# A two-layer decoder trunk on one core: two plain tile pairs per feed-forward instead of three, the rest as seven-product pairs

## The chip, the cores and the metric

One core of a Trainium2 chip runs the whole program. The metric is the device time of one execution in microseconds (us), the median of three runs. TensorE (PE) does the matmuls; VectorE (DVE) and ScalarE (ACT) make its operands and take its results; GpSimd (POOL) issues the transfers that add weights onto an SBUF tile; SyncE (SP) issues the plain loads.

## What is computed

528 tokens (16 learned ones ahead of 512) of 1024 channels go through two layers. In float32, per layer:

```python
for l in range(2):
    h = LN(a*h + 0.5*(silu(h @ wg1) * (h @ wu1)) @ wd1)
    z = h @ w_in
    y = concat(pool_mixer(z), gated_linear_attention(z)) @ w_out
    h = LN(a*h + y)
    h = LN(a*h + 0.5*(silu(h @ wg2) * (h @ wu2)) @ wd2)
```

Each feed-forward has 2816 hidden channels. The change touches the four feed-forwards alone.

## The kernel before

Everything is held transposed: channels on the 128 partitions, tokens along the free axis. x is 8 tiles of 128 channels (`KC`), the hidden side 22 tiles (`MT`). Tokens are worked on in two halves of 264 (`HALF`), in the last feed-forward 2 x 256, since there only the 512 real tokens count.

**Precision.** Each float32 operand is split in a high part, rounded to the matmul's type by a ScalarE copy, and a low part, the difference, taken by VectorE. A product is three matmuls: high x high, high x low, low x high.

**Weights** come as a stream of pieces of 128 x 1024, one for the gate and one for the up projection of a hidden tile, through raw buffers into four slots (`w_hi`, `w_lo`, `n % SLOTS`). SyncE loads a piece as soon as its buffer is free; ScalarE writes the high part (L1208) and, for the part whose low is made by a transfer, the negated high part (L1202), onto which GpSimd's transfer (L536) adds the raw weights. For the rest VectorE subtracts (L1695).

**Two ways to do a pair of a gate tile and an up tile.** Plain: 8 input tiles x 2 token halves x 3 matmuls x 2 = 96 matmuls of 264 columns; tiles 0 to 2 (`CLASSIC`) are made so. Seven-product: the gate and up weights and the two halves of channels and tokens make a 2 x 2 block matrix product, done by Winograd's form of Strassen's scheme with 7 block products in place of 8 (`fast_pair`): 7 x 4 tiles x 3 = 84 matmuls. They run in the order P1 (plain), P5, P6 (sums of weights times sums of x), P2 (plain), P7, P3, P4. Each needs additions besides. VectorE makes four sums of raw weights per pair (`w_sums`, `s_sum`), ScalarE and VectorE split them (`sum_high`, `sum_low`), and four sums of x per feed-forward (`v_sums`, `v_sum`; split by `v_high`, `v_low`). Of the running sums in PSUM, ScalarE copies P1 from one bank to the other (L1263, `p1_copied`); P6 may add onto its bank only after that. It also copies P5 (L1277) and the sum after P6 (L1282) to SBUF, and VectorE adds them back (L1753 after P7, L1766 after P3); P4 waits for the first of these adds. The down projection of the first 18 hidden tiles runs as twelve seven-product pairs (63 matmuls each), between the up pairs; for it VectorE makes four sums of each two hidden tiles (`t_sums`).

**Order.** Nothing is scheduled by a tool: each engine's program is written out, engines run in order, and semaphores hold them back. At the start of a feed-forward TensorE does tiles 0, 1 together (L619, L620, L645 as x arrives, then L655 to L657), then plain tile 2 (L609 to L611), then the pairs in `FAST_ORDER`. Meanwhile the layer norm before ends: VectorE's last step is the low part of x tile 7 (L1933), ScalarE's the full x (L1404), and x sums need all of it. `s_hi`, `s_lo` share memory with `v_sum`, so weight sums are split after the x sums.

## Time and profile before

| | |
|---|---|
| median of 3 runs | 1784.02 us (1783.56 to 1785.22) |
| span of the profiled execution | 1782.4 us |
| TensorE busy | 1770.1 us, 99% |
| VectorE busy | 1434.4 us, 80% |
| ScalarE busy | 1168.0 us, 66% |
| GpSimd busy | 340.0 us, 19% |
| DMA | 148 GB/s mean |

A timeline row gives start, duration, engine, line, operation, tiles written and read, shape, and how many instructions it merges; in brackets the idle time ahead of it and what ended that. Matmul ends are modelled, so their spacing, not their duration, tells the rate. L numbers are lines of the kernel before.

### The profile page before, as it was taken

The page shows a single profiled execution, that of the slowest core. Times are in us where ns is not written, and L with a number is a line of the kernel's source. Part 1 is how long each engine was busy: PE and PEld are TensorE (multiplying, and loading weights), DVE is VectorE, ACT ScalarE, POOL GpSimd, SP SyncE. Part 2 cuts the span into 40 slices and gives each one's busy share as a digit, 9 for nine tenths or more (in the row PEclk, how much of TensorE's full clock was granted, in tenths as well). Part 3 has the DMA queues.
Part 4 walks back from the last instruction along what each step waited for, and adds up shares of the span by engine and source line. Part 5 has one row for each costly group of instructions (what it writes and reads, how often), then busy time and mean ns, then how long its engine had stood idle before and what let it go on. Part 6 is the DMA issues. An engine that isn't in the chain of part 4 may idle for free.

```text
span 1782.4 us, 37725 instructions
## 1 busy us (share of the span) xinstructions
PE 1770.1 (99%) x14462; PEld 1733.0 (97%) x14462; DVE 1434.4 (80%) x2577; ACT 1168.0 (66%) x2047; POOL 340.0 (19%) x376
## 2 busy tenths in 40 slices
PE   9999999999999999999999999999999999999997
PEld 9999999999999999999999999999998889999996
DVE  7988888668568988888689888886785689888886
ACT  6767666574357667676576767665743577777764
POOL 2111212311011121111311111113110111111113
PEclk9999999999999999999999999999999999999999
DMA  7675766556565766766556757565665656767662
GB/s 217 141 183 129 177 141 144 150 137 141 115 138 110 170 167 148 169 138 159 145 138 145 176 129 180 134 155 139 141 142 117 147 126 149 185 133 185 133 166 72
DMA packets 112561, 263.54 MB, mean 148 GB/s; under 512 B 10752, under 2 KB 35328, under 8 KB 112384
## 3 DMA queue, kind: packets, MB, share of 16 engines
q1 hardware_dynamic: 66592, 167.86, 32.0%
q0 software_dynamic: 45504, 92.29, 30.8%
q8 instruction: 116, 1.90, 0.4%
q10 hardware_dynamic: 288, 0.98, 0.2%
q14 instruction: 61, 0.50, 0.1%
HBM read 259.00 MB, written 2.10 MB: 146 GB/s over the span
## 4 chain that ended last, share of the span: by engine, by line
PE 99%; DVE 0%; DMA 0%; ACT 0%; issue 0%; ACTq 0%; DVEq 0%
PE PS L680 21%; PE PS L682 21%; PE PS L681 21%; PE PS L655 5%; PE PS L656 4%; PE PS L657 4%; PE PS L609 3%; PE PS L611 3%; PE PS L610 3%; PE PS L619 2%; PE PS L645 2%; PE PS L620 2%; PE PS L987 2%; PE PS L808 1%; PE PS L875 0%; PE PS L902 0%
## 5 line engine op out<-in xcount | busy, mean ns | idle before, releaser
L536 POOL DMA_DIRECT2D w_lo<-in_stream x316 | 269.4, 853 | 1336.8 <-ACT w_lo L1202 1301.9
L1198 ACT ACTIVATE s_hi<-s_sum 128x512 fp32r<-128x512 f32 (+1 forms) x496 | 291.1, 588 | 154.2 <-PE PS L682 145.4
L1701 DVE TENSOR_TENSOR s_lo<-s_sum,s_hi 128x512 fp32r<-128x512 f32 (+1 forms) x496 | 294.4, 633 | 2.9 <-ACT s_hi L1198 2.6
L680 PE MATMUL PS<-v_hi,s_hi 128*128 128x264 f32 (+1 forms) x912 | 258.8, 284 | 0.0
L682 PE MATMUL PS<-v_hi,s_lo 128*128 128x264 f32 (+1 forms) x912 | 258.1, 283 | 0.0
L681 PE MATMUL PS<-v_lo,s_hi 128*128 128x264 f32 (+1 forms) x912 | 258.0, 283 | 0.0
L682 PE MATMUL PS<-x_hi,w_lo 128*128 128x264 f32 (+1 forms) x656 | 185.8, 283 | 0.0
L680 PE MATMUL PS<-x_hi,w_hi 128*128 128x264 f32 (+1 forms) x656 | 185.7, 283 | 0.0
L681 PE MATMUL PS<-x_lo,w_hi 128*128 128x264 f32 (+1 forms) x656 | 185.6, 283 | 0.0
L681 PEld LDWEIGHTS PS<-v_lo,s_hi 128*128 128x128 f32 x912 | 172.2, 189 | 0.0
L680 PEld LDWEIGHTS PS<-v_hi,s_hi 128*128 128x128 f32 x912 | 171.8, 188 | 0.0
L682 PEld LDWEIGHTS PS<-v_hi,s_lo 128*128 128x128 f32 x912 | 171.4, 188 | 0.0
L1208 ACT ACTIVATE w_hi<-raw 128x1024 fp32r<-128x1024 f32 (+2 forms) x152 | 147.1, 968 | 8.0 <-DMA raw<-in_stream 8.0
L1202 ACT ACTIVATE w_lo<-raw 128x512 fp32r<-128x512 f32 (+2 forms) x196 | 143.1, 730 | 0.0
L655 PE MATMUL PS<-x_hi,w_hi 128*128 128x264 f32 (+1 forms) x472 | 140.9, 299 | 0.1
L656 PE MATMUL PS<-x_lo,w_hi 128*128 128x264 f32 (+1 forms) x472 | 139.0, 295 | 0.0
L657 PE MATMUL PS<-x_hi,w_lo 128*128 128x264 f32 (+1 forms) x472 | 138.8, 294 | 0.0
L1263 ACT ACTIVATE PS<-PS 128x264 f32<-128x264 f32 (+1 forms) x124 | 46.3, 373 | 136.4 <-PE PS L682 136.4
L682 PE MATMUL PS<-x_hi,s_lo 128*128 128x264 f32 (+1 forms) x448 | 127.9, 286 | 0.0
L681 PE MATMUL PS<-x_lo,s_hi 128*128 128x264 f32 (+1 forms) x448 | 127.2, 284 | 0.0
L680 PE MATMUL PS<-x_hi,s_hi 128*128 128x264 f32 (+1 forms) x448 | 127.1, 284 | 0.0
L680 PEld LDWEIGHTS PS<-x_hi,w_hi 128*128 128x128 f32 x656 | 123.5, 188 | 0.0
(295 smaller groups left out, 5719.8 us busy)
## 6 DMA issues: line engine op xcount, KB each, us to landing
raw<-in_stream SPq DMA_DIRECT2D x164, 512.0 KB, 4.4
w_lo<-in_stream POOLq DMA_DIRECT2D x160, 256.0 KB, 4.6
spare<-in_stream SPq DMA_DIRECT2D x72, 512.0 KB, 6.8
w_lo<-in_stream POOLq DMA_DIRECT2D x60, 512.0 KB, 7.7
raw<-in_stream SPq DMA_DIRECT2D x48, 384.0 KB, 4.2
spare<-in_stream SPq DMA_DIRECT2D x48, 384.0 KB, 5.3
w_lo<-in_stream POOLq DMA_DIRECT2D x96, 192.0 KB, 4.8
X<-in_x_t SPq DMA_DIRECT2D x8, 264.0 KB, 5.8
```

The costliest lines, as they stand in the source:

```text
L536: pool.dma_start(w_lo[:, slot, to], stream[n // RAWS, n % RAWS, :, part], accum_op=ALU.add).then_inc(lo_added[slot], 16)
L609: nc.tensor.matmul(o, hi, rhs_hi[:, k, tok], start=first, stop=False)
L655: yield nc.tensor.matmul(o, hi, rhs_hi[:, k, tok], start=k == 0, stop=False)
L656: yield nc.tensor.matmul(o, hi, rhs_lo[:, k, tok], start=False, stop=False)
L657: yield nc.tensor.matmul(o, lo, rhs_hi[:, k, tok], start=False, stop=k == n - 1)
L680: nc.tensor.matmul(o, hi[:, w], r_hi, start=start and k == 0, stop=False, skip_group_check=True)
L681: nc.tensor.matmul(o, hi[:, w], r_lo, start=False, stop=False, skip_group_check=True)
L682: m = nc.tensor.matmul(o, lo[:, w], r_hi, start=False, stop=stop and k == last, skip_group_check=True)
L1198: nc.scalar.activation(s_hi[:, j - 1, w], s_sum[:, j - 1, w], ACT.Copy).then_inc(S["s_hi_done"], 1)
L1202: nc.scalar.activation(w_lo[:, n % SLOTS, to], of, ACT.Copy, scale=-1.0).then_inc(S["raw_neg"], 1)
L1208: nc.scalar.activation(w_hi[:, n % SLOTS, to], of, ACT.Copy).then_inc(S["raw_hi"], 1)
L1701: V.tensor_tensor(s_lo[:, j - 1, w], s_sum[:, j - 1, w], s_hi[:, j - 1, w].bitcast(F32), ALU.subtract).then_inc(S["s_lo_done"], 1)
```

## The change

`CLASSIC` goes from 3 to 2: tile 2 becomes the first up pair of the seven-product kind, and with it the slots, buffers and waits of all pieces shift by one pair. The x sums move to memory that later holds the hidden tiles (`v_sum_a`, `v_sum_b`), so that `s_hi` and `s_lo` no longer share with them. Sum 2 of x is taken with the other sign by a plain addition, and ScalarE's `scale=-1.0` and one VectorE instruction with two operations give its high and low parts the sign back. The order of both engines at the start of a feed-forward, up to the second pair, is written anew; the adds in PSUM of the first pair become `add_p5(0)` and `add_u2(0)` within it. The low parts of hidden tile 1 and its sums go to the second and third pair. Some `then_inc` that nobody waits for are dropped.

```diff
-BEHIND = 2
+BEHIND = 3
-CLASSIC = 3
+CLASSIC = 2
...
         with ExitStack() as s4:
-            v_sum = sb("v_sum", [P, 4, BAND, HALF], F32, s4)
+            s_hi = sb("s_hi", [P, 4, BLOCK], F32R, s4)
+            s_lo = sb("s_lo", [P, 4, BLOCK], F32R, s4)
...
+                v_sum_a = sb("v_sum_a", [P, 2, BAND, HALF], F32, s11)
...
+                v_sum_b = sb("v_sum_b", [P, 2, BAND, HALF], F32, s12)
...
# TensorE, ffn
                 product(3, 3, x_hi, x_lo, KC, span=span).then_inc(S["piece_done"], 1)
-                m = CLASSIC - 1
-                for j in range(2):
...
-                        for o, tok in matmul_parts(2 * (m % 2) + j, span):
-                            x = tile_products(o, tok, n % SLOTS, k, k, x_hi, x_lo, k == 0, k == KC - 1)
-                    x.then_inc(S["piece_done"], 1)
                 for i in range(FAST):
...
# ScalarE
-            def v_high(l, f, j, n):
+            def v_high(l, f, j, span):
 
                 act.wait_ge(S["v_sum_done"], 4 * (2 * l + f) + V_ORDER.index(j) + 1)
-                nc.scalar.activation(v_hi[:, j - 1, :, 0:n], v_sum[:, j - 1, :, 0:n], ACT.Copy).then_inc(S["v_hi_done"], 1)
+                nc.scalar.activation(v_hi[:, j - 1, :, 0:halved(span)[1]], v_sum(j, span), ACT.Copy,
+                                     scale=-1.0 if j == 2 else 1.0).then_inc(S["v_hi_done"], 1)
...
# ScalarE, ffn
+                v_high(l, f, 3, span)
+                v_high(l, f, 1, span)
                 act.wait_ge(S["piece_done"], FP + 1)
                 silu_of(0, span)
-                gate_high(FP + 4)
-                gate_negative(FP + 4)
-                v_high(l, f, V_ORDER[0], halved_n)
-                v_high(l, f, V_ORDER[1], halved_n)
+                gate_high(first)
+                gate_negative(first)
+                sum_high(l, f, 0, 1)
+                v_high(l, f, 2, span)
+                up_high(first + 1)
+                sum_high(l, f, 0, 2)
                 h_high(l, f, 0, span)
-                gate_high(FP + 5)
-                gate_negative(FP + 5)
+                v_high(l, f, 4, span)
+                sum_high(l, f, 0, 3)
                 act.wait_ge(S["piece_done"], FP + 3)
                 silu_of(2, span)
-                v_high(l, f, V_ORDER[2], halved_n)
-                v_high(l, f, V_ORDER[3], halved_n)
-                gate_high(first)
-                gate_negative(first)
-                h_high(l, f, 1, span)
-                up_high(first + 1)
-                sum_high(l, f, 0, 1)
-                sum_high(l, f, 0, 2)
-                act.wait_ge(S["piece_done"], FP + 5)
-                silu_of(0, span)
-                t_high(l, f, 1, span)
-                sum_high(l, f, 0, 3)
                 sum_high(l, f, 0, 4)
-                h_high(l, f, 2, span)
                 for i, (kind, a, b) in enumerate(FAST_ORDER):
...
+                    if i == 1:
+                        hidden_high(l, f, CLASSIC - 1, span)
...
# VectorE
                     elif j == 2:
                         dve.wait_ge(S["v_sum_done"], at + 1)
-                        x = V.scalar_tensor_tensor(out=v[1], in0=v[2], scalar=-1.0, in1=b11, op0=ALU.mult, op1=ALU.subtract)
+                        x = V.tensor_tensor(v_sum(2, span), v_sum(3, span), b11, ALU.add)
...
# VectorE, ffn
-                v_sums(l, f, span, (3, 1))
+                v_sums(l, f, span, (3, 1, 2))
+                w_sums(l, f, 0, (1, 3, 2))
                 classic_product(0)
-                gate_low(FP + 4)
+                v_low(l, f, span, 1)
+                sum_low(l, f, 0, 1)
+                gate_low(first)
+                w_sums(l, f, 0, (4,))
+                v_low(l, f, span, 2)
+                sum_low(l, f, 0, 2)
+                v_sums(l, f, span, (4,))
+                v_low(l, f, span, 3)
+                sum_low(l, f, 0, 3)
+                v_low(l, f, span, 4)
+                sum_low(l, f, 0, 4)
+                classic_product(1)
+
+                w_sums(l, f, 1, (1,))
+                gate_low(fast_piece(l, f, 1))
+                add_p5(0)
+                w_sums(l, f, 1, (3, 2))
+                sum_low(l, f, 1, 1)
+                add_u2(0)
+                sum_low(l, f, 1, 2)
+                w_sums(l, f, 1, (4,))
+                sum_low(l, f, 1, 3)
+                sum_low(l, f, 1, 4)
                 h_low(l, f, 0, span)
-                v_sums(l, f, span, (2, 4))
-                gate_low(FP + 5)
-                v_low(l, f, span, 1)
-                v_low(l, f, span, 2)
-                classic_product(1)
-                w_sums(l, f, 0)
-                gate_low(first)
-                v_low(l, f, span, 3)
...
+                t_sums(l, f, CLASSIC - 1, span)
                 for i, (kind, a, b) in enumerate(FAST_ORDER):
+                    if i == 0:
+                        continue
...
+                    if i == 1:
+                        h_low(l, f, CLASSIC - 1, span)
...
+                    if i == 2:
+                        t_low(l, f, CLASSIC - 1, span)
```

## Rows read from the trace of the kernel before

**Rows 1.** The page: span, busy time by engine, and the chain that ended last.
```profile
span 1782.4 us, 37725 instructions
PE 1770.1 (99%) x14462; PEld 1733.0 (97%) x14462; DVE 1434.4 (80%) x2577; ACT 1168.0 (66%) x2047; POOL 340.0 (19%) x376
...
PE 99%; DVE 0%; DMA 0%; ACT 0%; issue 0%; ACTq 0%; DVEq 0%
```

**Rows 2.** Windows: stretch, its length, busy time (count) by engine, granted clock, DMA share, GB/s.
```profile
40.56:326.17 285.61, 285.61 (x2355) 285.37 (x2354) 240.56 (x440) 195.87 (x382) 55.90 (x62) 1.00 0.67 155
28.96:40.56 11.60, 11.60 (x99) 11.60 (x97) 11.38 (x17) 9.22 (x14) 2.56 (x3) 1.00 0.75 161
1455.06:1466.18 11.12, 11.12 (x50) 9.02 (x48) 10.44 (x16) 8.53 (x13) 2.56 (x3) 1.00 0.77 150
1466.18:1746.03 279.85, 279.23 (x2354) 278.34 (x2353) 239.32 (x442) 195.16 (x384) 55.87 (x62) 1.00 0.67 159
```

**Rows 3.** Timeline of VectorE at the start of the second feed-forward.
```profile
560.27 1.25 DVE L1652 TENSOR_TENSOR v_sum<-X 128x1056 f32<-128x1056 f32 x1
561.44 1.25 DVE L1654 TENSOR_TENSOR v_sum<-X 128x1056 f32<-128x1056 f32 x1
...
570.91 2.42 DVE L1666 TENSOR_TENSOR v_lo<-v_sum,v_hi 128x1056 fp32r<-128x1056 f32 x2
573.25 0.70 DVE L1565 SCALAR_TENSOR_TENSOR h_raw<-PS,silu 128x528 f32<-128x528 f32 x1
...
576.24 0.68 DVE L1682 TENSOR_TENSOR s_sum<-raw 128x512 f32<-128x512 f32 x1
...
580.13 1.29 DVE L1701 TENSOR_TENSOR s_lo<-s_sum,s_hi 128x512 fp32r<-128x512 f32 x2
```

**Rows 4.** Timeline of ScalarE in the same stretch.
```profile
559.56 1.28 ACT L1160 ACT_TABLE_LOAD   x1
563.13 0.61 ACT L1160 ACTIVATE silu<-PS 128x528 f32<-128x528 f32 x1 [2.29 <-PE PS L645]
563.64 1.06 ACT L1208 ACTIVATE w_hi<-raw 128x1024 fp32r<-128x1024 f32 x1
564.59 0.62 ACT L1202 ACTIVATE w_lo<-raw 128x512 fp32r<-128x512 f32 x1
565.11 2.05 ACT L1190 ACTIVATE v_hi<-v_sum 128x1056 fp32r<-128x1056 f32 x2
```

**Rows 5.** Timelines of TensorE and ScalarE there: plain tile 2 begins; first P1 copy.
```profile
569.22 0.28 PE L609 MATMUL PS<-x_hi,w_hi 128*128 128x264 f32 x1
...
582.47 0.38 ACT L1263 ACTIVATE PS<-PS 128x264 f32<-128x264 f32 x1
```

**Rows 6.** Timeline of ScalarE in the mixer: a table load and what follows it.
```profile
385.17 1.28 ACT L1454 ACT_TABLE_LOAD   x1
386.46 1.09 ACT L1454 ACTIVATE ex<-ex 128x1056 f32<-128x1056 f32 x1
```

**Rows 7.** Timelines at the start of the first and of the last feed-forward.
```profile
17.16 1.25 DVE L1652 TENSOR_TENSOR v_sum<-X 128x1056 f32<-128x1056 f32 x1
...
22.87 0.61 ACT L1160 ACTIVATE silu<-PS 128x528 f32<-128x528 f32 x1 [7.22 <-PE PS L645]
...
1446.91 1.22 DVE L1652 TENSOR_TENSOR v_sum<-X 128x1024 f32<-128x1024 f32 x1
```

**Rows 8.** Timeline of TensorE in the last feed-forward's second pair.
```profile
1485.48 0.35 PE L680 MATMUL PS<-v_hi,w_hi 128*128 128x256 f32 x1 [0.41 <-issue]
```

**Rows 9.** Transfers issued from 560 to 600: tile, count, size, median us to landing.
```profile
spare<-in_stream SPq DMA_DIRECT2D x3, 512.0 KB, 6.6
```

**Rows 10.** Timeline of TensorE at either end, and a window (TensorE alone).
```profile
5.50 0.42 PE L620 MATMUL PS<-x_hi,w_lo 128*128 128x264 f32 x1
...
1771.42 1.11 PE L824 MATMUL PS<-ident,col_rstd 128*128 128x128 f32 x8
...
1777.00:1778.00 1.00, 0.00 (x0) 0.76 0.66 250
```

More of the change, by code:

```diff
@@ L163, in kind_of @@
     if r < 2 * CLASSIC or r >= LAST_DOWN:
-        return "first" if n < SLOTS else "added" if r < SLOTS else "half" if r < 2 * CLASSIC else "split"
+        return "first" if n < SLOTS else "added" if r < SLOTS else "split"
     return "up" if r % 2 else "gate"
@@ L207, in dma_adds @@
 def dma_adds(n):
-    return kind_of(n) in ("added", "half", "gate", "up")
+    return kind_of(n) in ("added", "gate", "up")
 def engine_splits(n):
-    return kind_of(n) in ("split", "half", "gate")
+    return kind_of(n) in ("split", "gate")
 def added_value(n):
@@ L356, in build @@
             silu = sb("silu", [P, T], F32, s4)
-        with ExitStack() as s5:
-            s_hi = sb("s_hi", [P, 4, BLOCK], F32R, s5)
-            s_lo = sb("s_lo", [P, 4, BLOCK], F32R, s5)
         with ExitStack() as s2:
@@ L372, in build @@
         with ExitStack() as s3:
+            with ExitStack() as s11:
+                sb("reserve_h", [P, 2 * T], F32, s11)
+                v_sum_a = sb("v_sum_a", [P, 2, BAND, HALF], F32, s11)
             h_hi = sb("h_hi", [P, 2 * THIRDS, T], F32R, s3)
@@ L381, in build @@
             h_raw = sb("h_raw", [P, 2 * THIRDS, T], F32, s3)
+            with ExitStack() as s12:
+                v_sum_b = sb("v_sum_b", [P, 2, BAND, HALF], F32, s12)
             t_raw = sb("t_raw", [P, 2, 4, HALF], F32, s3)
@@ L430, in norm_bias, with v_sum, x_blocks @@
             return par[:, c:c + 1]
+        def v_sum(j, span):
+            return (v_sum_a if j < 3 else v_sum_b)[:, (j - 1) % 2, :, 0:halved(span)[1]]
+        def x_blocks(span):
+            early, late = tokens(span, 0), tokens(span, 1)
+            return X[:, 0:BAND, early], X[:, 0:BAND, late], X[:, BAND:KC, early], X[:, BAND:KC, late]
         def t_block(main, x, k, span):
@@ L485, in raw_halves, with wait_x_full @@
             return [raw[:, buffer_of(n), low_half(n)], raw[:, buffer_of(n), high_half(n)]]
+        def wait_x_full(eng, l, f):
+            if l == 0 and f == 0:
+                for k in range(KC):
+                    eng.wait_ge(x_loaded[k], 16)
+            else:
+                eng.wait_ge(S["x_full_done"], (l * LN_PER + 2 * f) * (KC - EARLY))
+                eng.wait_ge(S["early_full"], (l * LN_PER + 2 * f) * EARLY)
         def wait_stream(eng, l, idx):
@@ L1665, in v_low @@
                 dve.wait_ge(S["v_hi_done"], 4 * (2 * l + f) + V_ORDER.index(j) + 1)
-                V.tensor_tensor(v_lo[:, j - 1, :, 0:n], v_sum[:, j - 1, :, 0:n], v_hi[:, j - 1, :, 0:n].bitcast(F32),
-                                ALU.subtract).then_inc(S["v_lo_done"], 1)
+                high = v_hi[:, j - 1, :, 0:n].bitcast(F32)
+                if j == 2:
+                    x = V.scalar_tensor_tensor(out=v_lo[:, 1, :, 0:n], in0=v_sum(2, span), scalar=-1.0, in1=high,
+                                               op0=ALU.mult, op1=ALU.subtract)
+                else:
+                    x = V.tensor_tensor(v_lo[:, j - 1, :, 0:n], v_sum(j, span), high, ALU.subtract)
+                x.then_inc(S["v_lo_done"], 1)
             def w_sums(l, f, i, js=S_ORDER):
@@ new lines, in add_u2 @@
+                def add_u2(i):
+                    i_all, ps = fast_index(l, f, i), bank_set(i)
+                    dve.wait_ge(S["p3_acc"], i_all + 1)
+                    dve.wait_ge(S["u2_copied"], i_all + 1)
+                    V.tensor_tensor(PS[ps][:, 1, 0:n], PS[ps][:, 1, 0:n], u2_copy[:, 0:n],
+                                    ALU.add).then_inc(S["c12_done"], 1)
+                v_sums(l, f, span, (3, 1, 2))
+                w_sums(l, f, 0, (1, 3, 2))
+                classic_product(0)
@@ L1743, in ffn @@
                         add_down(l, f, i - 1, span)
-                    elif was == "up":
-                        fast_prod(l, f, was_a, 2 - ps, span)
+                    else:
+                        fast_prod(l, f, was_a, bank_set(i - 1), span)
                     if follows:
@@ L1750, in ffn @@
                             sum_low(l, f, i + 1, 2)
[L1751 to L1754 removed]
+                    add_p5(i)
                     if i < BEHIND:
                         sum_low(l, f, i + 1, 2)
[L1757 to L1760 removed]
+                    if i == 1:
+                        h_low(l, f, CLASSIC - 1, span)
+                    if was == "up" and kind == "up":
                         h_low(l, f, was_a, span)
@@ L1763, in ffn @@
                         h_low(l, f, sum(PHASES[was_a]), span)
-                    dve.wait_ge(S["p3_acc"], i_all + 1)
-                    dve.wait_ge(S["u2_copied"], i_all + 1)
-                    V.tensor_tensor(PS[ps][:, 1, 0:n], PS[ps][:, 1, 0:n], u2_copy[:, 0:n],
-                                    ALU.add).then_inc(S["c12_done"], 1)
-                    if i == 0:
-                        t_low(l, f, 1, span)
-                    elif was == "up" and kind == "up":
+                    add_u2(i)
+                    if i == 2:
+                        t_low(l, f, CLASSIC - 1, span)
+                    if was == "up" and kind == "up":
                         t_low(l, f, was_a, span)
```

68 lines of the change are left out of this document (23 added, 45 removed).

## Prediction

> **What bounds the kernel now.** I read the page first: TensorE is busy for 99% of the span, the chain that ended last is 99% TensorE, while VectorE has 80% and ScalarE 66% [rows 1]. So time is the number of matmuls times their spacing, plus any pause in them. Next I took the windows of the parts that the change touches [rows 2]: a plain tile pair takes 11.60 us (96 matmuls of 264 columns), in the last feed-forward 11.12 us (48 of 512 columns); the part made of seven-product pairs holds 2352 matmuls (19 up pairs of 84 and 12 down pairs of 63; the windows count two or three more that run over their edges) in 285.61 us, which is 0.1214 us each, and in the last feed-forward 279.85 us. The timelines of VectorE and ScalarE at the start of the second feed-forward [rows 3, 4] show what must be ready before the first seven-product pair, and [rows 5] where TensorE is then: today it reaches the point that the change makes the new start of that pair at 569.22. I call the feed-forwards stages 1 to 4; in each the products of a pair run in the order P1, P5, P6, P2, P7, P3, P4.
>
> **What it removes from TensorE.** In each stage a plain pair becomes a seven-product pair. Stages 1 to 3: 84 x 0.1214 = 10.20 us in place of 11.60, 1.40 less each. Stage 4: of its pair part 279.23 us are busy (the idle rest is a pause, below), 0.1187 per matmul, 84 of them 9.97 us in place of 11.12, 1.15 less. Together 3 x 1.40 + 1.15 = 5.35 us. This is on the path, since nothing but TensorE is.
>
> **What the new start asks for.** The first pair begins one plain pair (11.6 us) earlier against the layer norm, but its operands can't begin earlier: the sums of x need all of X. I laid the new order of both engines onto the rows. VectorE begins the next instruction 0.08 us before the printed end when it waits for nothing (1.25 long, 1.17 to the next start), ScalarE 0.10 before (0.61 and 0.51) [rows 3, 4]. So VectorE pays 1.17 for a sum or low part of x (1056 columns), 0.61 for a weight sum or low part (512 columns), 0.62 for a product; ScalarE pays 0.98 for a high part of x, 0.96 for a gate's high part, 0.52 for a 512 column copy, 0.51 for silu, 0.3 for a 264 column copy (0.38 long, [rows 5]; the high part of tile 0 at the same). A signal between engines costs 0.04.
>
> Stage 2, VectorE from 560.27 [rows 3]: x sums 3, 1, 2 (3 x 1.17) to 563.78; weight sums 1, 3, 2 (3 x 0.61) to 565.61. ScalarE takes high parts 3 and 1 as they come, the second from 562.73 to 563.78. Then comes silu, and its table load is no longer hidden: today it runs at 559.56, ahead of silu's wait [rows 4]; now two copies stand before it. I price it at 1.28, as the load at 385.17 whose successor starts at 386.46 [rows 6]: silu runs 565.06 to 565.67. VectorE: product of tile 0 from 565.71 to 566.33, low part 1 of x to 567.50, low part of weight sum 1 (its high part ends at 567.67) from 567.71 to 568.32, gate's low half, done at 569.01. TensorE needs that at 569.22, so P1 isn't late. VectorE goes on at 568.93: weight sum 4, low part 2 of x, low part of sum 2 (1.17 + 2 x 0.61) to 571.32, and only then x sum 4, which ends at 572.57.
>
> **The wait it adds.** ScalarE's order is silu, gate high and negated, s_hi 1, v_hi 2, up high and negated, s_hi 2, h_hi 0, **v_hi 4**, s_hi 3, silu of tile 1, s_hi 4, and behind all of these the copy of P1 out of PSUM (L1263). v_hi 4 waits for x sum 4, and so does everything queued behind it. It starts at 572.61; then 0.98 + 0.52 + 0.51 + 0.52 give 575.14 for the P1 copy, done 575.52. TensorE has finished issuing P1 and P5 at 569.22 + 24 x 0.1214 = 572.13, and P6 adds onto the bank that is being copied, so it waits for that copy until 575.56. In the kernel before, this same copy starts at 582.47, right as P1 ends [rows 5], because ScalarE has nothing left to do. **A pause of 3.4 us.** Stage 3 has the same spacing of the same instructions: 3.4 us.
>
> Stage 1: VectorE is free for the sums at 17.16 [rows 7], early, and there is no table load; silu starts at 22.87 as now. The same addition from there (product 23.52, low part of sum 1 from 25.51, x sum 4 from 29.08 to 30.33, v_hi 4 from 30.37, copy from 32.9 to 33.3) against P5's end at 28.96 + 2.91 = 31.87 gives 1.4 us. Stage 4: VectorE starts at 1446.91 [rows 7] with 1024 column steps of 1.14; silu ends at 1452.27, the gate's low half at 1455.58, and TensorE arrives at 1455.06 [rows 2]: 0.6 us for P1; x sum 4 ends at 1459.05, the copy at 1461.94, P5's issue at 1458.46: 3.5 us. Together 4.1 us. The four stages: 1.4 + 3.4 + 3.4 + 4.1 = 12.3 us.
>
> **Bounds of this term.** The lower one is ScalarE's own work if x sum 4 were never late: 7.88 us of its list from 565.06, copy done 573.32, 1.2 us of pause in stages 2 and 3, none in stage 1, 1.3 + 0.6 in stage 4: 4.3 us. The upper one adds a slower table load and 0.1 for each of the dozen signals: 1 us more a stage, 16 us. I take 12.3, since each step has a row of the same engine and size. The rule that speaks against the load's price: the Trainium skill, ScalarE: Activation LUTs, section What ACT_TABLE_LOAD costs, puts a switch of table at the load of 1283 ns plus a drain of about 1380 ns. By that rule silu and what hangs on it would be 1.4 us later in three stages, and the sum 4.1 us larger; the rows with 385.17 and 386.46 [rows 6] have no room for a drain and disagree.
>
> **The second pair.** In stage 4 of the kernel before, P4 of the second pair pauses (0.41 us idle before one matmul [rows 8], 0.62 idle in the window [rows 2]), since VectorE reaches the PSUM add of P7 late: it carries the four sums of the hidden tile besides four weight sums. The change brings those four hidden sums to the first pair's tail in all stages. No row shows the new order; between 0 and the 0.6 of that row I take 0.3 a stage for stages 1 to 3, nothing new for stage 4: 0.9 us. From the third pair on VectorE has a pair's work as before (the low and hidden parts of tile 1 are spread over two pairs for that), and the following 30 pairs run as today.
>
> **Edits at nothing.** The x sum with two operands and the sign in v_hi 2 cost what they did (1.25 and 1.26 long); the weight sums' buffers moved onto the norm's only matter for races. The transfers move too: SyncE's loads for the second pair are issued once the first gate and up are negated, near 569.7, in one burst; a spare load takes 6.6 us to land [rows 9], so near 577, while VectorE asks for it at 577.2 behind the pause. Without the pause this cover would be gone and some tenths would show. GpSimd's adding transfer for the gate goes out near 567.2, before P2 at 573.6.
>
> **The sum.** -5.35 + 12.3 + 0.9 = +7.85 us. The profiled execution has a span of 1782.4 us, the median of the runs is 1784.02, 1.6 us more outside the first and last instruction, which the change doesn't touch: span 1790.3, median 1791.9.
>
> **Rivals.**
> 1. The P1 copy isn't held by x sum 4, only by ScalarE's own list (the lower bound). Against it: ScalarE is strictly in order in every row read, and the diff puts v_hi 4 ahead. -5.35 + 4.3 + 0.9 = -0.15: 1783.9, no change. Chance 0.08.
> 2. Nothing waits, and the shorter matmul list is the whole effect: -5.35 + 0.9, 1779.6, faster. For it speaks only the idle share of both engines; in this stretch it isn't theirs to use. It decides if the copy lands within 2.9 us of the pair's start. Chance 0.05.
> 3. The clock. The matmul at 5.50 lasts 0.42 us, later ones of its shape 0.28 [rows 5, 10]: at the start of the span the engine is still on the lower of its two levels, 1.2 and 2.4 GHz. And after its last work at 1771.42 + 1.11 the granted clock falls to its half within the window 1777 to 1778 (mean 0.76, so near 1777.5), after 5.0 us without work [rows 10]. The new pauses are 3.4 us. Should they suffice, each costs at most the 5.5 us at half speed that the start shows, 2.7 us: one to three of them 1794.6 to 1800.0, the middle 1797.3, slower. Chance 0.09. The Trainium skill says (TensorE: Matmul & The Clock Gate, section What's actually happening) that the throttled level is the default and that activity releases it; the trace agrees. No row shows whether 3.4 us is enough.
> 4. ScalarE stays shut for as long again after the table load, 1.28 us [rows 4], once the load isn't hidden: silu, the product and all behind it move by that in stages 2 to 4, 3 x 1.28 = 3.8, 1795.7, slower. The rows at 385.17 [rows 6] speak against it. Chance 0.02. The Trainium skill's drain, named above, is this mechanism.
>
> **How the numbers follow.** The forecast has 0.76; its own range, with each stage's pause off by 0.7 us at most, is 1789 to 1795. The range runs from 1788 to 1798: it takes in the middle of rival 3 and rival 4 and leaves out rivals 1 and 2 (0.13) and the tails. What a measurement of this kernel can tell from no change is about 0.2%, 3.6 us. Slower by more: 0.76 + 0.09 + 0.02 = 0.87; within: 0.08; faster: 0.05.
>
> **What the profile after should show.** TensorE has 14462 matmuls as before (12 fewer in three stages, 36 more in stage 4, where narrow ones take the place of wide ones). In the waits, TensorE's third product of the first pair waits for ScalarE's copy of P1, four times, the longest near 3.5 us; v_hi 4 waits for VectorE's x sum; the table load stands after two v_hi. VectorE gets 9 more instructions a stage. I am wrong if P6 follows P5 without a pause, if the copy of P1 starts before v_hi 4, if the granted clock drops inside a stage, or if more than a microsecond a stage is lost in the second pair.

## The result, and the profile after

The changed kernel takes 1796.84 us (median of four runs, 1794.44 to 1797.16), the kernel before, run beside it, 1783.79: ratio 1.0068, 95% interval 1.0054 to 1.0082. It is slower by 13.05 us. The forecast was +7.85, to 1791.9; the time lies inside the stated range and 4.9 us above the point. It is above the 1789 to 1795 that the prediction named as the forecast's own range; the stated one reaches further because it was drawn to take in rival 3, the clock.

The page of the kernel after: span, busy time by engine, the chain that ended last. They answer to [rows 1].

```profile
span 1794.9 us, 37845 instructions
PE 1771.5 (99%) x14462; PEld 1734.2 (97%) x14462; DVE 1452.7 (81%) x2613; ACT 1178.0 (66%) x2075; POOL 341.6 (19%) x376
...
PE 93%; DVE 3%; ACT 3%; issue 1%; DMA 0%; ACTq 0%; DVEq 0%
```

The count of matmuls is the same, VectorE has 36 instructions more, and the chain, 99% TensorE before, now passes through VectorE and ScalarE for 6% of the span. The share of 99% for TensorE hides that: it is an average over 1.8 ms, and the loss sits in four places. The waits of TensorE name them (who waits, for whom, us in total, times, the longest):

```profile
PE PS L701 <- ACT PS L1265: 11.0, 4, 3.2
PE PS L1161 <- DVE ones_mean L2255: 1.1, 1, 1.1
PE PS L701 <- DVE w_lo L1701: 0.6, 1, 0.6
```

L1265 is the copy of P1 (L1263 before), waited for once in each feed-forward; L1701 is the gate's low half, at P1 of stage 4; the middle line belongs to the start of the kernel and is the same in the kernel before (1.1 us). In the second feed-forward the timeline of TensorE shows the end of P5, the pause, and the first matmuls of P6:

```profile
572.56 0.29 PE L703 MATMUL PS<-v_hi,s_lo 128*128 128x264 f32 x1
576.10 0.59 PE L701 MATMUL PS<-v_hi,s_hi 128*128 128x264 f32 x1 [3.25 <-ACT PS L1265]
576.48 0.42 PE L702 MATMUL PS<-v_lo,s_hi 128*128 128x264 f32 x1
576.70 0.42 PE L703 MATMUL PS<-v_hi,s_lo 128*128 128x264 f32 x1
576.92 0.42 PE L701 MATMUL PS<-v_hi,s_hi 128*128 128x264 f32 x1
```

From start to start the gap is 3.53 us where 0.12 is usual, so the pause costs 3.41. Then there is something that the forecast left out: the matmuls that follow stand 0.22 us apart, not 0.12. The timeline of ScalarE over the same stretch is what [rows 4] became:

```profile
564.35 1.28 ACT L1170 ACT_TABLE_LOAD   x1
565.64 0.61 ACT L1170 ACTIVATE silu<-PS 128x528 f32<-128x528 f32 x1
...
570.68 0.41 ACT L1182 ACTIVATE h_hi<-prod 128x264 fp32r<-128x264 f32 x1
573.14 1.08 ACT L1200 ACTIVATE v_hi<-v_sum_b 128x1056 fp32r<-128x1056 f32 x1 [2.05 <-DVE v_sum_b L1661]
574.13 0.61 ACT L1209 ACTIVATE s_hi<-s_sum 128x512 fp32r<-128x512 f32 x1
574.65 0.59 ACT L1170 ACTIVATE silu<-PS 128x528 f32<-128x528 f32 x1
575.14 0.62 ACT L1209 ACTIVATE s_hi<-s_sum 128x512 fp32r<-128x512 f32 x1
575.66 0.38 ACT L1265 ACTIVATE PS<-PS 128x264 f32<-128x264 f32 x1
```

ScalarE stands still for 2.05 us at v_hi 4, which waits for x sum 4, and makes three more instructions before the copy. VectorE, the counterpart of [rows 3], made that sum behind the low parts of x and of weight sum 2:

```profile
570.09 1.25 DVE L1669 SCALAR_TENSOR_TENSOR v_lo<-v_sum_a,v_hi 128x1056 fp32r<-128x1056 f32 x1
571.26 0.68 DVE L1707 TENSOR_TENSOR s_lo<-s_sum,s_hi 128x512 fp32r<-128x512 f32 x1
571.86 1.25 DVE L1661 TENSOR_TENSOR v_sum_b<-v_sum_a,X 128x1056 f32<-128x1056 f32 x1
```

Last, windows of TensorE alone (stretch, length, busy and count, granted clock, DMA share, GB/s). The first four are one stretch of stage 3: before the pause, in it, the first microsecond after it, and what follows. The other two lie in stages 2 and 4.

```profile
924.50:926.20 1.70, 1.70 (x16) 1.00 0.70 136
926.30:929.30 3.00, 0.02 (x1) 1.00 0.91 249
929.40:930.50 1.10, 0.94 (x7) 1.00 1.05 395
930.70:933.90 3.20, 3.20 (x16) 0.50 0.98 292
...
575.70:578.90 3.20, 2.80 (x12) 0.50 1.04 390
...
1470.00:1473.20 3.20, 2.81 (x13) 0.50 1.03 381
```

The granted clock fell to the lower of its two levels, 1.2 GHz, in three of the four feed-forwards, each time for 3.4 us by the clock's own records (575.61 to 579.03, 930.60 to 934.01, 1469.90 to 1473.32). In stage 3 it fell a microsecond after the matmuls had resumed at full speed. In stage 1, whose pause is 1.4 us, it stayed up. These are the falls of the profiled execution. The four executions aren't alike in this: three have a mean granted clock of 0.995 and take 1796.7 to 1797.2 us, the fourth has 0.997 and takes 1794.44, so it spent less time at the lower level.

### Where the 13.05 us are

I took the starts of the matmuls of each seven-product pair and counted what they take beyond the usual spacing (0.121 us, in stage 4 0.118); I call this a pair's surplus.

| us | forecast | measured |
|---|---|---|
| matmul time taken out | -5.35 | -5.35 (count as forecast) |
| pause before P6, stages 1 to 4 | 1.4, 3.4, 3.4, 3.5 | 1.44, 3.41, 3.41, 3.38 |
| P1 of stage 4 | 0.6 | 0.78 |
| second pairs | 0.9 | 1.7 (0.5 in each of stages 1 to 3, 0.1 more than before in stage 4) |
| half clock | 0 | 4.6 (1.5, 1.7, 1.5: the first pair's surplus less its pause) |
| sum | +7.85 | +13.4 |

The price of a fall follows from the spacing: the 3.4 us at half clock hold some 13 to 16 matmuls 0.22 apart that would otherwise stand 0.12 apart. The measured column is read from the profiled execution, whose span is 12.5 us longer than the one before (1794.9 against 1782.4), so it counts 0.9 us too much. 0.3 of that the kernel before loses too, at the start of its own first pair in stage 4; the rest is time that TensorE gained ahead of the first pairs (0.2 us in stage 1, 0.4 in stage 4), for which there is no term. And of the 4.6 us of half clock 0.5 aren't the clock's: the kernel with the filled pause, below, has a surplus of 0.1 to 0.2 us beyond each of these pauses with the clock up. The falls alone cost 4.1 us (1.3, 1.5, 1.3).

### The profile page after: what moved, and what is told of

The parts are those of the page before. It is cut to its first block, busy times and chain, and to the rows that moved or that the text cites. A ratio compares the mean times of both kernels' runs of the same rounds, so it can differ in the third digit from the quotient of the medians.

```text
span 1794.9 us, 37845 instructions
## 1 busy us (share of the span) xinstructions
PE 1771.5 (99%) x14462; PEld 1734.2 (97%) x14462; DVE 1452.7 (81%) x2613; ACT 1178.0 (66%) x2075; POOL 341.6 (19%) x376
## 4 chain that ended last, share of the span: by engine, by line
PE 93%; DVE 3%; ACT 3%; issue 1%; DMA 0%; ACTq 0%; DVEq 0%
PE PS L701 22%; PE PS L702 22%; PE PS L703 22%; PE PS L676 4%; PE PS L677 4%; PE PS L678 4%; PE PS L630 3%; PE PS L632 3%; PE PS L631 3%; PE PS L997 2%; PE PS L666 1%; PE PS L640 1%; PE PS L641 1%; PE PS L818 1%; ACT X L1411 0%
## 5 line engine op out<-in xcount | busy, mean ns | idle before, releaser
L1209 ACT ACTIVATE s_hi<-s_sum 128x512 fp32r<-128x512 f32 (+1 forms) x512 | 300.7, 589 | 168.3 <-PE PS L703 139.8
L1707 DVE TENSOR_TENSOR s_lo<-s_sum,s_hi 128x512 fp32r<-128x512 f32 (+1 forms) x512 | 306.1, 634 | 5.6 <-ACT s_hi L1209 4.8
L701 PE MATMUL PS<-v_hi,s_hi 128*128 128x264 f32 (+1 forms) x960 | 274.7, 286 | 11.1 <-ACT PS L1265 11.0
L702 PE MATMUL PS<-v_lo,s_hi 128*128 128x264 f32 (+1 forms) x960 | 272.7, 284 | 0.0
L703 PE MATMUL PS<-v_hi,s_lo 128*128 128x264 f32 (+1 forms) x960 | 272.7, 284 | 0.0
L701 PE MATMUL PS<-x_hi,w_hi 128*128 128x264 f32 (+1 forms) x688 | 195.5, 284 | 0.6 <-DVE w_lo L1701 0.6
L702 PE MATMUL PS<-x_lo,w_hi 128*128 128x264 f32 (+1 forms) x688 | 195.0, 283 | 0.0
L701 PEld LDWEIGHTS PS<-v_hi,s_hi 128*128 128x128 f32 x960 | 181.9, 189 | 13.4 <-ACT PS L1265 12.4
L702 PEld LDWEIGHTS PS<-v_lo,s_hi 128*128 128x128 f32 x960 | 182.3, 190 | 0.0
L703 PEld LDWEIGHTS PS<-v_hi,s_lo 128*128 128x128 f32 x960 | 181.6, 189 | 0.0
L676 PE MATMUL PS<-x_hi,w_hi 128*128 128x264 f32 (+1 forms) x472 | 140.8, 298 | 0.1
L677 PE MATMUL PS<-x_lo,w_hi 128*128 128x264 f32 (+1 forms) x472 | 138.9, 294 | 0.0
L1265 ACT ACTIVATE PS<-PS 128x264 f32<-128x264 f32 (+1 forms) x128 | 47.8, 373 | 133.8 <-PE PS L703 133.8
```

What stands on the lines that cost most here:

```text
L676: yield nc.tensor.matmul(o, hi, rhs_hi[:, k, tok], start=k == 0, stop=False)
L677: yield nc.tensor.matmul(o, hi, rhs_lo[:, k, tok], start=False, stop=False)
L701: nc.tensor.matmul(o, hi[:, w], r_hi, start=start and k == 0, stop=False, skip_group_check=True)
L702: nc.tensor.matmul(o, hi[:, w], r_lo, start=False, stop=False, skip_group_check=True)
L703: m = nc.tensor.matmul(o, lo[:, w], r_hi, start=False, stop=stop and k == last, skip_group_check=True)
L1209: nc.scalar.activation(s_hi[:, j - 1, w], s_sum[:, j - 1, w], ACT.Copy).then_inc(S["s_hi_done"], 1)
```

## The experiments

Each experiment is the changed kernel with the edit shown; the later ones build on earlier ones, as their expectations say. The theory to be tested: two things make the loss, a wait chain (x sum 4 on VectorE, v_hi 4 on ScalarE, the P1 copy queued behind it, P6) and, on top of it, the clock. The rivals: ScalarE's own list is the bound whatever VectorE does; or the extra 5 us are not the clock.

### The copy moved ahead of the blocked instruction

```diff
                 h_high(l, f, 0, span)
+                copy_p1(0)
                 v_high(l, f, 4, span)
```

> The changed kernel with one move on ScalarE: the first pair's P1 copy goes ahead of the high part of x sum 4. Theory (everything queued behind that high part waits for x sum 4): P6 no longer pauses, but the copy after P6 is still behind it, so P7 pauses instead, by ScalarE's list (x sum 4 ends 3.4 us after P1's start, then 0.98 + 0.52 + 0.51 + 0.52 + 0.95 + 0.52 + 0.3 + 0.4 gives 8.1, and P7 is due at 5.8) 2.2 us in stages 2 to 4 and 0.7 in stage 1. A pause of 2.2 us leaves the granted clock at full: 1796.8 - 0.7 - 3 x 1.2 - 4.6 = 1788 us; with the clock still falling, up to 1792.7. Rival (the P1 copy was the only late one): no pause anywhere in the first pair, 1781.5 us.

Measured: 1790.67 us, ratio 1.0038 (1.0024 to 1.0053). That is 6.2 us under the changed kernel, 2.7 above the 1788 that was expected and inside the bound of 1792.7 for a clock that still falls. P6 no longer waits, but four new waits of up to 2.1 us stand at P7 (the waits of TensorE, and its timeline there):

```profile
PE PS L701 <- ACT u_copy L1290: 6.8, 4, 2.1
...
576.93 0.39 PE L701 MATMUL PS<-v_hi,s_hi 128*128 128x264 f32 x1 [2.03 <-ACT u_copy L1290]
```

The copy was the immediate holder and v_hi 4 the true one: with the copy out of its way, v_hi 4 and all that is queued behind it still come late, and the next product that needs something from that queue (the u2 copy, which is ScalarE's copy of the sum after P6) pays two thirds of the old price. The clock fell three times in the profiled execution here too (1791.73 us, mean clock 0.995), after pauses of only 2.2 us. Three of the five executions have a mean clock of 0.997 or 0.998 and take 1790.2 to 1790.7 us, so the same pauses don't end in a fall every time.

### The late sum made earlier

```diff
                 w_sums(l, f, 0, (4,))
+                v_sums(l, f, span, (4,))
                 v_low(l, f, span, 2)
                 sum_low(l, f, 0, 2)
-                v_sums(l, f, span, (4,))
```

> The changed kernel with one move on VectorE: x sum 4 goes ahead of the low parts of x 2 and weight sum 2. Theory (x sum 4 holds the P1 copy): its high part starts 1.8 us earlier, the copy ends 4.6 us after P1's start, so P6 pauses 1.65 us in stages 2 to 4 in place of 3.4 and not at all in stage 1, the clock doesn't fall, 1785.8 us. Rival (ScalarE's own work or its table load makes the pause, x sum 4 merely stands there): pauses stay at 3.4 and 1.4, 1796.8 us.

Measured: 1787.73 us, ratio 1.0021 (1.0012 to 1.0031), 9.1 us under the changed kernel. The pauses before P6 fall from 3.4 to 1.6, and in stage 1 the pause goes altogether. The clock never fell, and all ten executions have a mean clock of 0.998 or 0.999. This shows that in the changed kernel's order x sum 4 is the head of the chain, and it comes near the floor as well: with the sum in time, 1.6 us are left because v_hi 4, two high parts and a silu still stand before the copy. It missed its expectation by 2 us: new waits for the u2 copy came up (1.8 us in two) and a longer second pair in stage 2. ScalarE's timeline in stage 3:

```profile
924.77 0.38 ACT L1265 ACTIVATE PS<-PS 128x264 f32<-128x264 f32 x1
927.36 1.06 ACT L1219 ACTIVATE w_hi<-raw 128x1024 fp32r<-128x1024 f32 x1 [2.21 <-DMA raw<-in_stream]
```

The next pair's gate, loaded in one burst with three other pieces, landed late, and the copies are queued behind its high part. The prediction had said that some tenths of this would show once the pause that covers it is gone; it was more.

### The pause filled with unread matmuls

This one leaves every wait where it is and puts matmuls of 128 columns into the time in which TensorE waits. Their result is never read.

```diff
+                if i == 0:
+                    for _ in range(5 if l + f == 0 else 14):
+                        nc.tensor.matmul(PS[ps + 1][:, 1, 0:P], ones_mean[:, :], ones_mean[:, :], start=True, stop=True)
                 pe.wait_ge(S["p1_copied"], i_all + 1)
```

> The changed kernel, with small matmuls that nobody reads between P5 and P6 of each stage's first pair, 5 in stage 1 and 14 in the others (0.213 us each), into a part of PSUM that is overwritten later. The wait for the P1 copy stays. Theory (the 5 us above the forecast are TensorE at half clock after the pauses): P6 starts when it did, the clock stays full, 1796.8 - 4.6 = 1792.2 us, ratio to the kernel before 1.0047. Rival (those 5 us are lost in the second pair or in transfers): no change, 1796.8 us, ratio 1.0073.

Measured: 1792.62 us, ratio 1.0049 (1.0034 to 1.0064), 4.2 us under the changed kernel and 0.4 above the expectation. Timeline, and windows over the three places:

```profile
572.48 3.29 PE L748 MATMUL PS<-ones_mean 128*128 128x128 f32 x28
...
572.00:580.00 8.00, 7.92 (x68) 1.00 0.97 298
923.00:932.00 9.00, 8.91 (x76) 1.00 0.97 273
1463.00:1473.00 10.00, 9.90 (x86) 1.00 0.93 257
```

The same wait, the same product late, and a granted clock of 1.00 throughout. 4.2 of the 4.9 us that the forecast missed are thus the clock, and 1792.6 is close to the 1791.9 that the forecast gave without it.

### The table load hidden again

```diff
+                nc.scalar.preload_act_table(ACT.Silu)
                 v_high(l, f, 3, span)
```

> The changed kernel with the table for silu loaded ahead of the high parts of x 3 and 1, where ScalarE waits anyway. Theory (the load costs its 1.28 us and no drain, and VectorE's own list nearly covers it): the product of tile 0 starts 0.16 us earlier, the low part of weight sum 1 0.36, so the pauses in stages 2 to 4 shrink by 0.4 each, 1795.7 us. Rival (a drain of about the load's length comes with a load that isn't hidden): 1.3 us or more per stage, 1792.5 us or less. Second rival: the load is never on the path, 1796.8 us.

Measured: 1795.03 us, ratio 1.0062 (1.0047 to 1.0077). The load at 560.50 is done 0.7 us before v_hi 3 can start, silu comes a microsecond sooner, and since x sum 4 stays bound to VectorE the pause shrinks only from 3.41 to 3.05 in stages 2 and 3, as expected; in stage 4 it is P1 that starts 0.45 sooner. The expectation named an end of 1792.5 for the case that more than the load stands in front of silu; the time is above it. That it lies within 0.7 us of the expected 1795.7 is in part chance, because the expectation had no term for the clock: the four executions range from 1792.34 us at a mean clock of 0.997 to 1797.45 at 0.994. In the profiled one the clock fell in stages 3 and 4, after pauses of 3.03 and 3.4 us, and stage 2 kept it after 3.05 (TensorE's timeline there; P6 resumes at the usual spacing):

```profile
576.12 0.39 PE L701 MATMUL PS<-v_hi,s_hi 128*128 128x264 f32 x1 [2.89 <-ACT PS L1266]
576.34 0.29 PE L702 MATMUL PS<-v_lo,s_hi 128*128 128x264 f32 x1
576.47 0.28 PE L703 MATMUL PS<-v_hi,s_lo 128*128 128x264 f32 x1
```

### The burst of loads spread

The early sum, and SyncE holds the third pair's gate load until P6 of the first pair is done.

```diff
+                if kind_of(n) == "gate" and place_of(n)[2] == 2:
+                    sp.wait_ge(S["p6_acc"], fast_index(*place_of(n)[:2], 0) + 1)
```

> e2's order on VectorE, and SyncE holds the gate load of the third pair until P6 of the first pair is done, so that the burst of loads is spread. Theory (the pauses before P7 that e2 still has, 0.9, 0.7 and 1.4 us, come from a gate load that lands late in a burst of four and that ScalarE waits for ahead of its copies): these go, the pauses of 1.6 us before P6 stay, and the time is 1785.9, some 1.8 us under e2. Rival (the transfers are not the cause, or the held load now comes too late itself): 1787.7 as e2, or above.

Measured: 1787.72 us, ratio 1.0019 (1.0010 to 1.0028): no change against 1787.73. In the trace the waits for the u2 copy fell from 1.8 to 1.0 us (at P7 of stages 1 and 3, start to start, from 0.93 and 1.44 to 0.66 and 0.93), but they did not vanish, and the median doesn't show it. The load is late also without the fourth transfer beside it (in stage 3 it landed after 5.6 us in place of 6.1). That the burst is the cause isn't shown.

### Both lists woven by a guess at what is needed next

On ScalarE all three copies of the first pair between the high parts; on VectorE also the loop over the second and third pair reordered, so that PSUM additions come before weight sums that seemed not due. The silu table is loaded ahead, the first gate's low part comes right behind product 0, the second silu goes behind the fourth sum's high part, and x sum 4 stays where the change has it, behind the low parts of x 2 and weight sum 2. Of the edit, the loop:

```diff
# VectorE, the loop over pairs
+                    if i == 1:
+                        w_sums(l, f, 2, (1, 3))
+                        add_p5(1)
+                        fast_prod(l, f, was_a, bank_set(0), span)
+                        gate_low(fast_piece(l, f, 2))
+                        w_sums(l, f, 2, (2, 4))
+                        sum_low(l, f, 2, 1)
```

> ScalarE's and VectorE's lists of the first pairs woven by need: on ScalarE the P1 copy, the P5 copy and the u2 copy of pair 0 stand between v_hi 4 and the third and fourth sums' parts, and the silu table is loaded ahead; on VectorE the first gate's low part comes right behind product 0, and in the pairs 1 and 2 the P5 addition and the product come before the sums that are not due. Theory (the pauses are these lists' order and no more): 0.5 to 0.8 us of pause per stage remain against 1.4 us of TensorE work taken out, no fall of the clock, 1781.5, ratio to the kernel before 0.9985. Rival (a pause of 1 us or more comes up at another product in each stage, as in e1 and e2): 1785 to 1788.

Measured: 1808.84 us, ratio 1.0136 (1.0122 to 1.0150), outside both expectations. The waits of TensorE, and its timeline in the third pair of stages 1 and 2:

```profile
PE PS L701 <- ACT PS L1244: 16.9, 8, 2.4
...
57.30 0.39 PE L701 MATMUL PS<-v_hi,s_hi 128*128 128x264 f32 x1 [2.31 <-ACT PS L1244]
57.53 0.29 PE L702 MATMUL PS<-v_lo,s_hi 128*128 128x264 f32 x1
57.66 0.28 PE L703 MATMUL PS<-v_hi,s_lo 128*128 128x264 f32 x1
...
602.16 0.39 PE L701 MATMUL PS<-v_hi,s_hi 128*128 128x264 f32 x1 [2.31 <-ACT PS L1244]
602.39 0.31 PE L702 MATMUL PS<-v_lo,s_hi 128*128 128x264 f32 x1
602.51 0.40 PE L703 MATMUL PS<-v_hi,s_lo 128*128 128x264 f32 x1
602.71 0.42 PE L701 MATMUL PS<-v_hi,s_hi 128*128 128x264 f32 x1
```

The first pair is now free of pauses (0.15 us beyond the usual spacing in each stage), the second and third each wait 2.1 to 2.5 us for their P1 copy. In both, that copy stands on ScalarE behind the next gate's high part and high parts of weight sums, and VectorE now makes those sums later; in the third pair of stage 2 ScalarE had stood still for 4.09 us at one of them. It is the same kind of chain one pair further on, made by my edit. These rows also speak on the clock: the same idle time of 2.31 us (2.5 beyond the usual spacing) ends in half clock in stages 2 to 4 and not in stage 1.

The free first pair says more than the total. Its x sum 4 is as late as in the changed kernel: it starts 1.75 us after P1, there 2.12. Timelines of TensorE, VectorE and ScalarE in stage 2: P1 begins, x sum 4, the copy of the sum after P6, and P7, which begins as soon as P2 has been issued.

```profile
573.78 0.28 PE L701 MATMUL PS<-x_hi,w_hi 128*128 128x264 f32 x1
...
575.53 1.25 DVE L1679 TENSOR_TENSOR v_sum_b<-v_sum_a,X 128x1056 f32<-128x1056 f32 x1
...
578.69 0.38 ACT L1258 ACTIVATE u_copy<-PS 128x264 f32<-128x264 f32 x1
...
579.62 0.36 PE L701 MATMUL PS<-v_hi,s_hi 128*128 128x264 f32 x1
```

So with the copies in this order and the table loaded ahead, a late x sum 4 costs the first pair nothing. Whether the second pair then has to pay isn't separated here: the reordered loop and the later weight sums came in the same edit, and this first pair with the changed kernel's own loop was not run.

> e7 with the third pair's gate load held on SyncE as in e5. Theory (ScalarE no longer waits for that load ahead of its copies): within 0.5 us of e7. If the burst still delays a load that ScalarE needs early: up to 1.8 us under e7.

The same with the load held: 1808.10 us, ratio 1.0133 (1.0119 to 1.0146), 0.7 us lower, which the interval can't tell from none. The hold is worth nothing here either. In its profiled execution the clock fell in stage 2 after the second pair's pause of 2.05 us and not after the third pair's of 2.5, the other way round than without the hold.

### Only the first pair's copies by need

From the early sum; the loop over the later pairs is the change's own.

```diff
                 h_high(l, f, 0, span)
+                copy_p1(0)
                 v_high(l, f, 4, span)
                 sum_high(l, f, 0, 3)
                 act.wait_ge(S["piece_done"], FP + 3)
                 silu_of(2, span)
                 sum_high(l, f, 0, 4)
+                copy_p5(0)
+                copy_u2(0)
```

> e2's order on VectorE (token sum 4 before token low part 2), and on ScalarE the copies of pair 0 each where its product ends: the P1 copy before v_hi 4, the P5 copy behind the third sum's high part, the u2 copy behind the fourth sum's, all before the next pair's gate, whose load may be late. The pairs behind it keep the order of the change. Theory (in e1 v_hi 4 came too late for P7 because its sum did, in e2 the P1 copy came too late for P6 because v_hi 4, two high parts and a silu stood before it, in e7 the woven loop of the pairs 1 and 2 cost the time): no pause over 0.4 us in the first pairs but the 0.8 us before P1 of stage 4, the second pairs keep their 0.5 us of small waits, so 1783.8 - 5.35 + 0.8 + 2.1 = 1781.4, faster than before by 0.13%. Rival (this many things on ScalarE can't all be in time, a pause of over 1 us comes up at a product behind P6): 1785 to 1788.

Measured: 1787.47 us, ratio 1.0019 (1.0010 to 1.0028). The theory fell and the rival's 1785 to 1788 holds the time: P6 still waits 0.5 us in stages 2 to 4, and P4, a product behind it, 0.7 to 1.0. VectorE's timeline in stage 2, where P6 began at 572.89 in place of 572.38:

```profile
569.77 1.25 DVE L1678 TENSOR_TENSOR v_sum_b<-v_sum_a,X 128x1056 f32<-128x1056 f32 x1
570.94 1.25 DVE L1686 SCALAR_TENSOR_TENSOR v_lo<-v_sum_a,v_hi 128x1056 fp32r<-128x1056 f32 x1
572.11 0.68 DVE L1724 TENSOR_TENSOR s_lo<-s_sum,s_hi 128x512 fp32r<-128x512 f32 x1
```

P6 needs this low part of weight sum 2, which ends at 572.79. Moving x sum 4 ahead took ScalarE's queue off the path and put VectorE's on it. The woven kernel, which leaves x sum 4 behind this low part and loads the table ahead, has no wait here, so the first pair doesn't need the early sum in every order.

> e9 with the third pair's gate load held on SyncE as in e5. Theory: the copies no longer stand behind the late gate load, so the hold is worth nothing: within 0.5 us of e9. Rival: the late gate load still delays the second pair in stage 2 and 3, and the hold takes 0.5 to 1.5 us off e9.

With the hold: 1787.39 us, ratio 1.0018 (1.0009 to 1.0027), within 0.1 of the one without it, as the theory said of the time. In the trace P4 waits longer than without the hold (1.4 and 1.3 us in stages 3 and 4) and the second pair of stage 1 is 0.35 us shorter, so that the hold does nothing at all isn't shown.

### The whole start earlier

The kernel of the section before, without the hold, and the table load ahead.

```diff
+                nc.scalar.preload_act_table(ACT.Silu)
                 v_high(l, f, 3, span)
```

> e9 with the silu table loaded ahead of v_hi 3 and v_hi 1. Theory (ScalarE is no longer late in the first pair): within 0.5 us of e9. Rival (ScalarE is still what is late): 0.3 to 0.4 us off in each of three stages, 1 us under e9; the clock stays up in both.

Measured: 1783.79 us, ratio 0.9998 (0.9989 to 1.0007): level with the kernel before, and 3.7 us under the same without the edit. The theory fell, and the rival's 1 us is too small. The waits of TensorE:

```profile
PE PS L701 <- ACT PS L1244: 1.9, 4, 0.7
...
PE PS L701 <- DVE s_lo L1725: 0.4, 1, 0.4
...
PE PS L701 <- DVE w_lo L1719: 0.2, 1, 0.2
```

The same edit was worth 1.8 us in the changed kernel, part of it a fall of the clock that didn't come, and 3.7 here. VectorE's list runs from product 0, which waits for silu. Against the start of P1 in stage 2, x sum 4 begins 0.41 us sooner than without the edit, and the low part of weight sum 2 ends 0.42 sooner, at 2.97 us from that start where P6 is due at 2.91. So in stage 2 the wait at P6 goes, and the one at P4 with it, while stage 3 keeps 0.4 us at P4 and stage 4 0.55 at P6 and 0.4 at P4: the first pair's surplus falls from 1.55 to 0.26 us in stage 2 and from 1.77 to 0.82 in stage 3. In stage 2 of the changed kernel the same 0.4 us came off one wait of 3.4 and nothing else.

### The second pair's copy

```diff
-                    if i > 0 and follows:
+                    if i > 1 and follows:
                         gate_high(nxt)
                     if i > 0:
                         copy_p1(i)
+                    if i == 1:
+                        gate_high(nxt)
```

> e11 and one line more: in the second pair ScalarE makes the P1 copy before the next gate's high part, which takes 1.04 us and stands between that product's end and its copy. Theory (the 0.8 to 0.9 us waits before P6 of the second pair, 0.5 in stage 1, come from that order alone): they fall by about 0.7 us in each of the three later stages and by 0.4 in the first, 1783.8 - 2.5 = 1781.3, faster than the kernel before by 0.15%. Rival (something else is late by then, a low part on VectorE): the wait stays or moves to the next product, 1783.0 to 1784.

Measured: 1783.62 us, ratio 0.9997 (0.9988 to 1.0006). The rival: the wait before P6 went, and one at P7 took its place. TensorE's timeline in stage 2, of the kernel without and then of the one with this edit:

```profile
582.43 0.39 PE L701 MATMUL PS<-v_hi,s_hi 128*128 128x264 f32 x1 [0.48 <-ACT PS L1244]
```

```profile
585.56 0.39 PE L701 MATMUL PS<-v_hi,s_hi 128*128 128x264 f32 x1 [0.86 <-ACT u_copy L1258]
```

The second pair's surplus is 1.09 us without the edit and 1.17 with it.

> e12, and on VectorE the first gate's low part comes before token low part 1 and the first sum's low part. Theory (P1 of stage 4 waits 0.3 us for this low part, the last piece it needs): that wait goes and the rest stays, 0.3 us under e12, about 1781.0. Rival (v_lo 1 or the first sum's low part is then late for P5): e12's time or up to 0.5 us more.

With the first gate's low part ahead on VectorE: 1784.00 us, ratio 0.9998 (0.9989 to 1.0007). The wait at P1 of stage 4 is gone from the trace, worth 0.3 us, and the medians can't show so little.

## Why the prediction was right, and where it fell short

**The direction and the chain.** Right, and shown by two opposite edits. Moving the copy moved the wait to P7; making the sum early halved it. The rows stand as laid out: the stage began 0.52 us later against the profile of before, and x sum 4 (571.86), v_hi 4 (573.14) and the P1 copy (575.66) all lie within 0.05 us of the forecast's times plus 0.52. For an in-order engine the length to next start of each instruction, read from rows with no idle time, was enough.

**The pause term**, 12.3 us, measured 12.4 with P1 of stage 4 (0.6 forecast, 0.78 found).

**The floor of that term**, 1.2 us for stages 2 and 3 if x sum 4 were never late: with the early sum, which is nearly that case (ScalarE waited 0.28 us for it in stage 3), the pauses were 1.6. In the changed kernel the sum was late in all four stages, so rival 1 fell, and rival 2 with it.

**The table load**, 1.28 us and no drain: 564.35 + 1.28 = 565.63, silu at 565.64. Rival 4 fell. The Trainium skill's drain (ScalarE: Activation LUTs, section What ACT_TABLE_LOAD costs) is not in this trace in any place; the instruction behind the load starts 0.01 us after its end in stages 2 to 4.

**The second pair**, 0.9 us, was too small: 1.7. The step that was off is "0.3 a stage between 0 and 0.6"; stages 1 to 3 show 0.5 each, close to the row that bounded it, and stage 4 another 0.1. The changed stretch after the first pair of stage 1, in the form of [rows 2] (stretch, length, busy, clock), is 286.45 us for two matmuls more than the 285.61 of before:

```profile
40.25:326.70 286.45, 286.45 (x2357) 1.00 0.67 153
```

**The clock** is the step that was weighed wrong. It stood in the text as rival 3 with 0.09, since the only fall that the trace of before shows came after 5.0 us without work, and the pauses were to be 3.4. It happened in three of four stages of the profiled execution and costs 4.1 to 4.6 us; filling the pause took 4.2 back. A granted clock that drops inside a stage was one of the prediction's own signs of being wrong, and it is this sign that came. Its price was named too high (up to 2.7 each; 1.3 to 1.7 found). Its 1794.6 to 1800.0 holds the time, but that the middle is half a microsecond off is luck: it stood for two falls of 2.7, and there were three of about 1.5. Without a fall the terms as measured give -5.35 + 12.4 + 1.7 = 8.75, 1792.8 us, and the kernel with the filled pause takes 1792.62; that is the part that was foreseen. A single fall after 5.0 us is no evidence that 3.4 is safe; the chance should have been near one half. The Trainium skill (TensorE: Matmul & The Clock Gate, section Why this matters for your kernels) lists idle gaps between bursts of matmuls as what drops throughput in the middle of a kernel. The trace agrees, with half clock after three pauses of 3.4 us, and by that rule this rival would have been a likely case.

**Edits at nothing.** The sign and the buffers cost nothing that shows. The loads did once the pause had gone: ScalarE waited 2.21 us for one in stage 3 of the kernel with the early sum, where "some tenths" was said.

**Why the 5.35 us were not won.** The best versions have the same matmul list and are level with the kernel before: 1783.79, 1783.62 and 1784.00 us, which the medians can't tell apart. By the spacing of the matmuls in the first of them, 6.8 us are still lost in the first two pairs of the four stages (0.9, 1.4, 2.0, 2.6), where the kernel before loses 0.9, so about what was taken out. The plain pair that the change removed was the cover under which VectorE and ScalarE got ready. The woven kernel shows first pairs that lose next to nothing in all four stages (0.15 us each); whether they can be had without a loss in the second pair isn't settled.

## What to carry to other kernels

When a stretch of the bounding engine's work is taken out, ask what the other engines did under it, and lay their in-order lists onto rows before counting the gain. A wait blocks everything queued behind it: moving one victim ahead hands the wait to the next one, so look for the head of the chain and for everything that stands behind it, and expect the other engine's list to bind next. In these runs a pause of 2 us or more in TensorE could cost another 1.3 to 1.7 us by the clock, in some executions and not in others, so weigh that case in earnest.

## What the runs showed of the hardware

- The granted clock fell to 1.2 GHz for 3.4 us at a time. In the profiled executions it fell after pauses (beyond the usual spacing) of 3.4 us (four of four: three in the changed kernel, one with the table ahead), 3.03 us (stage 3, table ahead), 2.2 us (three of three, copy ahead), 2.5 us (five of eight third pairs of the two woven kernels) and 2.05 us (one of their eight second pairs). It stayed at 1.00 after 3.05 us (stage 2, table ahead), after the other 2.5 and 2.1 us pauses of the woven kernels, and after all pauses up to 1.6 us. So the length of a pause alone doesn't set it; what else does stays open.
- The fall came between 0.5 us before and 1.5 us after the matmuls resumed (930.60 against 929.56 in stage 3 of the changed kernel, 929.34 against 927.80 with the table ahead).
- One fall cost 1.4 to 1.7 us of a pair's surplus, 1.3 to 1.5 against the kernel with the filled pause.
- A silu table load of 1.28 us had nothing behind it but the next instruction, 0.01 us after its end.
- Loads issued together landed one after the other: in the changed kernel four of 512 KB, issued within 2 us of each other in stage 2, landed after 4.8, 7.0, 7.7 and 8.3 us. Between 560 and 600 us of the kernel before, the median was 3.9 for raw buffers and 6.6 for the spare ones [rows 9]. The two kinds alternate in the four. What makes the later ones slower isn't shown.
